# Seven-product gate and up: weight loads a tile further ahead of the hidden stores, another order of activation sums, and the second down chunk's loads amid h's

## What is computed

```python
h = h + mixed @ w_out[l]
u = rmsnorm(h, ln2_g[l])
h = h + (jax.nn.silu(u @ w_ffn_gate[l]) * (u @ w_ffn_up[l])) @ w_ffn_down[l]
```

## Time and profile before

| | us |
|---|---|
| median of 3 runs (2720.54 to 2722.23) | 2721.73 |
| the profiled execution's own time | 2721.55 |
| its span, first to last instruction | 2719.7 |
| TensorE busy | 2539.5 |
| VectorE busy | 1730.8 |
| GpSimd busy | 1062.1 |
| ScalarE busy | 944.5 |

### The profile page before, as it was taken

How to read it: one execution, slowest core, us unless ns; L and a number is a source line. 1 busy time by engine, 2 the same in 40 slices (tenths; PEclk the granted TensorE clock), 3 DMA queues, 4 the chain that set the end, 5 groups by cost and what they waited for, 6 DMA issues and landing times. The chain is left out here.

```text
span 2719.7 us, 32247 instructions
## 1 busy us (share of the span) xinstructions
PE 2539.5 (93%) x12772; PEld 1995.1 (73%) x12772; DVE 1730.8 (64%) x1757; ACT 944.5 (35%) x1380; POOL 1062.1 (39%) x555
## 2 busy tenths in 40 slices
PE   7999998998999989899999999899979999989998
PEld 5777765676777777688877777566867777777887
DVE  7777368557676666555667753965577766665554
ACT  6344156624333332100234331854243323320003
POOL 2000431156665566433520023121656655654333
PEclk9999999998999999999999999999999999999999
DMA  5010200032222322422220111002322232224221
GB/s 179 24 40 15 54 22 1 27 129 70 70 70 75 89 70 70 183 95 102 101 64 15 41 40 38 5 1 83 103 62 70 70 91 72 70 86 178 106 96 63
DMA packets 208295, 193.24 MB, mean 71 GB/s; under 512 B 31249, under 2 KB 180881, under 8 KB 208146
## 3 DMA queue, kind: packets, MB, share of 16 engines
q1 hardware_dynamic: 208146, 191.17, 22.3%
HBM read 147.11 MB, written 44.04 MB: 70 GB/s over the span
## 5 line engine op out<-in xcount | busy, mean ns | idle before, releaser
L2128 DVE TENSOR_TENSOR h<-ps,h 128x1024 f32<-128x1024 f32 x176 | 214.3, 1223 | 205.7 <-PE ps L228 191.4
L1972 POOL TENSOR_TENSOR w_a<-w_raw,w_a 128x512 fp32r<-128x512 f32 x110 | 187.7, 1731 | 371.0 <-ACT w_a L1962 371.0
L228 PE MATMUL ps<-u_hi,w_hi 128*128 128x512 f32 x896 | 295.8, 412 | 27.6 <-DVE f L872 13.3
L228 PE MATMUL ps<-u_hi,w_lo 128*128 128x512 f32 x896 | 280.0, 394 | 0.0
L228 PE MATMUL ps<-u_lo,w_hi 128*128 128x512 f32 x896 | 279.9, 394 | 0.0
L211 POOL TENSOR_TENSOR w_hi<-w_raw,ones 128x1024 fp32r<-128x1024 f32 (+1 forms) x37 | 70.2, 1898 | 482.9 <-DMA w_raw<-w_in 231.5
L2011 PE MATMUL ps<-u_b,w_a 128*128 128x512 f32 x1056 | 253.7, 389 | 0.0
L2011 PE MATMUL ps<-u_t,w_s 128*128 128x512 f32 x1056 | 246.5, 389 | 0.0
L2011 PEld LDWEIGHTS ps<-u_b,w_a 128*128 128x128 f32 x1056 | 198.2, 188 | 41.2
L2011 PEld LDWEIGHTS ps<-u_t,w_s 128*128 128x128 f32 x1056 | 198.2, 188 | 41.1
L228 PEld LDWEIGHTS ps<-u_hi,w_hi 128*128 128x128 f32 x896 | 164.0, 191 | 73.1 <-issue 24.0
(11 more groups left out here) (372 smaller groups left out, 5038.1 us busy)
## 6 DMA issues: line engine op xcount, KB each, us to landing
w_raw<-w_gate SPq DMA_DIRECT2D x44, 512.0 KB, 4.4
w_raw<-w_up SPq DMA_DIRECT2D x44, 512.0 KB, 5.5
hidden_spill<-hidden_gate SPq DMA_DIRECT2D x44, 512.0 KB, 3.3
w_raw<-w_down SPq DMA_DIRECT2D x44, 512.0 KB, 4.4
hidden_back<-hidden_spill SPq DMA_DIRECT2D x44, 512.0 KB, 4.1
w_raw<-w_in SPq DMA_DIRECT2D x42, 512.0 KB, 3.8
h_spill<-h SPq DMA_DIRECT2D x32, 512.0 KB, 4.7
h<-h_spill SPq DMA_DIRECT2D x32, 512.0 KB, 7.5
```

The lines of the kernel that those rows point to most:

```text
L228: last = nc.tensor.matmul(ps[:, bank0 + half, :], a, b[:, half * HALF:(half + 1) * HALF], start=(k == order[0] and n == 0), stop=(k == ord ...
L1972: nc.gpsimd.tensor_tensor(lo, src, hi.bitcast(F32), ALU.subtract).then_inc(w_lo, 1)
L2128: nc.vector.tensor_tensor(wide(h[:, m, :]), pair(p), wide(h[:, m, :]), ALU.add)\
```

## The change

The loads of tile i+1 move from behind the store of tile i-1 to ahead of it: the order is now load 1, load 2, store 0, load 3, store 1, and so on. A load waits for four low parts of the tile before. S3 moves to the second place of the weight order. The raws of T3 and T2 lie in the buffers of the hidden gate and up (`TRAW`), and VectorE makes T3's low parts, in another order of all activation sums. W is split from C22. At the end of the tiles, down chunk 0 is loaded ahead of the store of tile 20, the loads of chunk 1 stand after four of h's eight blocks, the last store behind all of h, and VectorE's low parts of chunk 0's hidden rows ahead of C11 of the last tile.

```diff
-        W_ORDER = ["A11", "A12", "A22", "S3", "S1", "S2", "S4"]
+        W_ORDER = ["A11", "S3", "A12", "A22", "S1", "S2", "S4"]
...
+        TRAW = [x[:, half * HALF:(half + 1) * HALF] for x in (GA, UP) for half in range(2)]
...
-                    sp.wait_ge(w_lo, 7 * i if i == 1 else 7 * (i - 1) + 3)
+                    sp.wait_ge(w_lo, 7 * i if i == 1 else 7 * (i - 1) + 4)
...
-            def dve_c22(dve, i):
+            def dve_w(dve, i):
                 dve.wait_ge(p_done, product_at(i, "P7"))
                 dve.wait_ge(v_copied, i + 1)
                 nc.vector.tensor_tensor(WT[:, :], ps[:, bank(i, "P7"), :], VC[:, :], ALU.add).then_inc(w_summed, 1)
+
+            def dve_c22(dve, i):
                 dve.wait_ge(w_summed, i + 1)
```

SyncE's program:

```diff
-                    for i in range(1, TILES):
+                    for i in range(1, 3):
                         load_weights(sp, i, 0)
                         load_weights(sp, i, 1)
-                        store_hidden(sp, i - 1)
-                    load_down(sp, 0)
+                    for i in range(3, TILES + 1):
+                        store_hidden(sp, i - 3)
+                        if i < TILES:
+                            load_weights(sp, i, 0)
+                            load_weights(sp, i, 1)
+                        else:
+                            load_down(sp, 0)
+                    store_hidden(sp, TILES - 2)
                     load_hidden(sp, 0)
-                    store_hidden(sp, TILES - 1)
                     sp.wait_ge(p_done, 7 * TILES)
                     for k in range(KT):
+                        if k == 4:
+                            load_down(sp, 1)
+                            load_hidden(sp, 1)
                         sp.dma_start(h[:, k, :], h_rows[k]).then_inc(h_back[k // 2], 16)
-                    for c in range(1, CHUNKS):
+                    store_hidden(sp, TILES - 1)
+                    for c in range(2, CHUNKS):
```

GpSimd in tile 0:

```diff
-                    pool_weight(pool, 0, W_ORDER0[5])
-                    for k in range(4):
-                        hi, lo, lo_raw = U_AT["T3"][k]
-                        pool.wait_ge(u_hi, U_HI_AT["T3", k])
-                        pool.wait_ge(u_dve, U_DVE_AT["T2 raw", k])
-                        nc.gpsimd.tensor_tensor(lo, lo_raw, hi.bitcast(F32), ALU.subtract).then_inc(u_pool, 1)
-                    pool_weight(pool, 0, W_ORDER0[6])
+                    for name in W_ORDER0[5:7]:
+                        pool_weight(pool, 0, name)
```

ScalarE in tile 0:

```diff
                     u_part("B21", 3)
+                    u_part("B22", 0)
+                    u_part("B22", 1)
                     norm_act(act, norm2, KT - 1, SQ2, None, None)
-                    act_weight(act, 0, W_ORDER0[5])
-                    for k in range(4):
-                        u_part("B22", k)
+                    for name in W_ORDER0[5:7]:
+                        act_weight(act, 0, name)
+                    u_part("B22", 2)
+                    u_part("B22", 3)
+                    act_p5(act, 0)
                     act_p1(act, 0)
-                    act_p5(act, 0)
-                    for k in range(4):
-                        u_part("T3", k)
-                    act_weight(act, 0, W_ORDER0[6])
-                    for name in ("T2", "T4"):
+                    for name in ("T3", "T2"):
                         for k in range(4):
                             u_part(name, k)
                     act.wait_ge(proj_done, J_OUT + KT + 1)
                     norm_rs(act, 0, (rs_part, 1))
+                    for k in range(4):
+                        u_part("T4", k)
+                    act_v(act, 0)
                     act.wait_ge(h_spilled, 16 * KT)
-                    for name in W_ORDER[0:3]:
-                        act_weight(act, 1, name)
-                    act_v(act, 0)
-                    for name in W_ORDER[3:7]:
+                    for name in W_ORDER:
                         act_weight(act, 1, name)
```

VectorE in tile 0 and in the turns after it (the activation parts of T3 and T2 also take their raws from `TRAW`, and `u_ready` waits on VectorE's count for all names):

```diff
-                    for k in range(4):
-                        u_part("T3 raw", k)
-                        u_part("T2 raw", k)
-                    for k in range(4):
-                        u_part("B22", k)
-                    dve_c11(dve, 0)
-                    for name in ("T4 raw", "T2", "T4"):
+                    for name in ("T3 raw", "B22", "T3", "T2 raw", "T2", "T4 raw"):
                         for k in range(4):
                             u_part(name, k)
-                    dve_sums(dve, 1, S_ORDER)
+                    u_part("T4", 0)
+                    u_part("T4", 1)
+                    dve_w(dve, 0)
+                    u_part("T4", 2)
+                    u_part("T4", 3)
+                    dve_sums(dve, 1, S_ORDER[0:1])
+                    dve_c22(dve, 0)
+                    dve_c11(dve, 0)
+                    dve_sums(dve, 1, S_ORDER[1:4])
                     dve.wait_ge(rstd_ready, 1)
-                    dve_c22(dve, 0)
                     dve_c12(dve, 0)
                     for i in range(1, TILES):
                         dve_c21(dve, i - 1)
                         if i + 1 < TILES:
                             dve_sums(dve, i + 1, S_ORDER)
+                        dve_w(dve, i)
                         dve_c22(dve, i)
+                        if i + 1 == TILES:
+                            dve_hidden(dve, 0)
                         dve_c11(dve, i)
                         dve_c12(dve, i)
-                        if i + 1 == TILES:
-                            dve_hidden(dve, 0)
```

More of the change, by code:

```diff
@@ L1804, in build @@
                  ("B11", 3), ("T1 raw", 3), ("T1", 2), ("B21", 0), ("T1", 3), ("B21", 1), ("B21", 2), ("B21", 3)] + \
-                [(b, k) for k in range(4) for b in ("T3 raw", "T2 raw")] + \
-                [(b, k) for b in ("B22", "T4 raw", "T2", "T4") for k in range(4)]
+                [(b, k) for b in ("T3 raw", "B22", "T3", "T2 raw", "T2", "T4 raw", "T4") for k in range(4)]
         U_DVE_AT = {x: n + 1 for n, x in enumerate(U_DVE)}
@@ L1974, in u_ready @@
             def u_ready(pe, name, k):
[L1975 to L1978, removed]
+                pe.wait_ge(u_dve, U_DVE_AT[name, k])
             def pe_product(pe, i, name):
@@ L2340, in u_part @@
                         scale = ln2(k) if name == "T1" else 1.0
-                        nc.scalar.activation(hi, lo_raw, ACT.Copy, scale=scale).then_inc(u_hi, 1)
+                        src = TRAW[k] if name in ("T3", "T2") else lo_raw
+                        nc.scalar.activation(hi, src, ACT.Copy, scale=scale).then_inc(u_hi, 1)
                     nc.scalar.activation(GSQ[0][:, :], YA[:, 0, :], ACT.Square).then_inc(group_sq[0], 1)
@@ L2449, in u_part @@
                             dve.wait_ge(u_hi, U_HI_AT["UG", k])
-                            nc.vector.scalar_tensor_tensor(lo_raw, h_part(k + 4, 1), ln2(k + 4),
+                            nc.vector.scalar_tensor_tensor(TRAW[k], h_part(k + 4, 1), ln2(k + 4),
                                                            h_part(k, 1), ALU.mult, ALU.subtract).then_inc(u_dve, 1)
                         elif name == "T2 raw":
-                            dve.wait_ge(u_dve, U_DVE_AT["T3 raw", k])
-                            nc.vector.scalar_tensor_tensor(lo_raw, h_part(k, 0), ln2(k),
-                                                           U_AT["T3"][k][2], ALU.mult, ALU.add)\
+                            dve.wait_ge(u_dve, U_DVE_AT["T3", k])
+                            nc.vector.scalar_tensor_tensor(TRAW[k], h_part(k, 0), ln2(k),
+                                                           TRAW[k], ALU.mult, ALU.add)\
                                 .then_inc(u_dve, 1)
@@ L2459, in u_part @@
                             nc.vector.scalar_tensor_tensor(lo_raw, h_part(k + 4, 0), ln2(k + 4),
-                                                           U_AT["T2"][k][2], ALU.mult, ALU.subtract)\
+                                                           TRAW[k], ALU.mult, ALU.subtract)\
                                 .then_inc(u_dve, 1)
@@ L2467, in u_part @@
                             dve.wait_ge(u_hi, U_HI_AT[name, k])
-                            dve.wait_ge(u_dve, U_DVE_AT["T4 raw", k])
-                            nc.vector.tensor_tensor(lo, lo_raw, hi.bitcast(F32), ALU.subtract)\
+                            if name == "T4":
+                                dve.wait_ge(u_dve, U_DVE_AT["T4 raw", k])
+                            nc.vector.tensor_tensor(lo, TRAW[k] if name in ("T3", "T2") else lo_raw, hi.bitcast(F32), ALU.subtract)\
                                 .then_inc(u_dve, 1)
```

1 line of the change is left out of this document (removed).

## The result

The changed kernel takes 2605.83 us (median of 4 runs, 2604.51 to 2606.77) against 2721.98 us for the one before on the same chip: 0.9573 of it, 95% interval 0.9556 to 0.9590, or 116.2 us less. The forecast was 2607.5. The profiled execution took 2604.51 us.

The account below looks back on a forecast made before the run. A ring through the hidden store and the next loads, not TensorE, was taken to set the steady tiles' pace. 71.8 + 14.5 + 27.7 = 114.0 us off 2721.5 gave 2607.5; range 2592 to 2638 us.

Parts of the forecast that it names:

- Part 1: Steady tiles of both layers: loads issued ahead of stores make TensorE the bound at 19.04 us a tile; 71.8 us off.
- The ring: Steady tiles: product, store, load, landing, split, P5 copy, P3, P4, product sets the pace, 20.9 and 21.0 us a tile.
- Part 2: Tile 0: operands made in a new order start P3 and P4 earlier; 6.9 and 7.6 us by layer, 14.5 together.
- The open choice: Tile 0: whether VectorE waits when it comes second to GpSimd; waits taken, gain 6.9 us, otherwise about 10.
- Part 3: Tile 21 and first down chunks: waits and slow matmuls behind them go; 27.7 us off, bounds 15 and 30.
- All three waits: TensorE's waits, layers one/two: W at P4 of tile 21 1.7/0.8, chunk 0 3.4/3.3, chunk 1 6.9/6.0 us.
- (a): Steady tiles: the stall moves to W, P4 waits 0.7 us in each of 40 tiles; about 2636 us; chance 0.12.
- (b): Tile 0 and down start find new waits of the old size, only steady tiles gain; 2650 us; chance 0.07.
- (c): Tile 0 loses nearly all its waits and no transient follows; 130 us off, 2592 us; chance 0.06.
- (d): Steady tiles: load's loop of landing, sums, splits, issue exceeds 20.9 us; about 2803 us at 24 a tile; chance 0.02.
- (e): Steady tiles: the reordering brings no earlier loads, P5's copy stays late; 2679 us; chance 0.03.
- the other doubt: Unbroken run of matmuls: the granted clock might fall there; none expected, no size or chance given.

Follow-up runs that it names:

- first run: Kernel before, with only each tile's loads moved ahead of the store of the tile before: 2642.3 us, 0.9706 of before.
- second run: Changed kernel with only the loads put back behind the store of the tile two before: 2692.4 us, 86.6 more.
- third and fourth run: Third: changed kernel with tile 0 as before, 2617.9 us. Fourth: changed kernel with the start of down as before, 2632.3 us.
- the dose after P7: Changed kernel with each load from i = 3 on also waiting for P7 of the next tile: 2641.4 us, 35.6 more.
- the wait for seven splits: Changed kernel with each load waiting for all seven low parts of the tile before instead of four: 2618.6 us, 12.8 more.
- after P1: Changed kernel with each load from i = 3 on also waiting for P1 of the next tile: 2606.7 us, 0.8 more.

## Why the prediction was right

**Part 1, loads ahead of stores: forecast 71.8, measured 72.5** from P1 of tile 1 to P1 of tile 21. The ring named in the prediction was the bound: its order alone gives the pace (first run) and takes it away (second run). The floor of 19.04 us was met to the hundredth, so the steady part is 75.8 as summed. The layout within the tile held: loads at +10.5 us (forecast +11.6), W at +11.8 (+12.4). The product ended at +3.4, not +5, because GpSimd did not hold VectorE there. The transient was charged with 2 us a layer; it is 1.6 (20.67 and 20.70 us in tile 1), P3 waiting for P5's copy as said; that is the whole 0.7.

**Part 2, tile 0: forecast 14.5, measured 14.3** (6.3 and 8.0 against 6.9 and 7.6). In the changed kernel's timeline of tile 0:

```profile
637.42 2.72 POOL L269 TENSOR_TENSOR acc<-acc,sq 128x1024 f32<-128x1024 f32 x1 [2.22 <-ACT sq L257]
...
637.80 4.59 DVE L2453 SCALAR_TENSOR_TENSOR hidden_up<-h,vectors 128x512 f32<-128x512 f32 x2
...
644.20 0.70 PE L2007 MATMUL ps<-u_b,w_hi 128*128 128x512 f32 x2 [2.90 <-DVE u_b L2446]
...
658.95 1.19 PE L2007 MATMUL ps<-u_t,w_hi 128*128 128x512 f32 x2 [2.94 <-DVE w_sum L2044]
```

P1 starts 0.72 us later in this trace than before, so 644.20 is 643.5 on the old clock (forecast 643.6), and P1 of tile 1 at 663.32 is 662.6 (662). The open choice is settled: the last two T3 raws took 4.59 us beside GpSimd's accumulation and splits where a free one takes 0.7, so the second one to come does wait. The rule of the Trainium skill ("SBUF — State Buffer", "Who interferes with whom") and this trace agree.

**Part 3, the start of down: forecast 27.7, undoing it costs 26.5.** All three waits went. The margin at chunk 1 is as worked out: its last weight part is ready at 1084.53, 2.1 us ahead of its first matmul. By the traces alone the stretch gained about 30 us (26.6 in the table and most of the 3.7 below it). The prediction put all of it down to the new start of down; the first run shows that the order of the loads gives 5.9 us of it by itself. So the total is right, and the split between parts 1 and 3 is a few us off.

**The rivals.** (a), a stall that moves to W: W is done 3.9 us ahead of P4 (810.70 against 798.23 + 16.32). (b), no gain in tile 0 and down: undoing them costs 12.1 and 26.5 us (third and fourth run). (c): tile 0's waits did not vanish, the bounds of part 2 were wide. (d), the longer ring: landings would have to be 12 us; even the dose after P7 stays below the kernel before. (e), loads no earlier: they leave 10.5 us into the tile instead of 6.4 us into the next. The clock stayed at full over the unbroken stretch, which was the other doubt; the stretch view of 340 us in the middle, busy times per engine, then the granted clock:

```profile
700.00:1040.00 340.00, 340.00 (x1502) 281.53 (x1501) 214.45 (x215) 118.97 (x198) 188.42 (x127) 1.00 0.25 82
```

The sum came out 2.2 us low (114.0 against 116.2). By the spans it is 3.1 (117.1): part 1 was 0.7 us better than its term, part 3 2.6 us, part 2 0.2 us worse.

## What to carry to other kernels

When an engine's wait repeats in every tile, follow it around until it closes; if the ring passes through an in-order queue where a transfer stands behind a later result for no need, moving that one line gives the whole gain of the steady tiles (79.8 of 116.2 us here), and nothing else in the tile has to change. Then measure how late the transfer may be: here 9.2 us into a tile was free, 11.0 was not, and the wait for seven splits cost 12.8 us through one load per layer, that of tile 2. What is freed in a ramp is partly handed back in the next tile, so the parts of such a change do not simply add: the order is worth 79.8 us alone and 86.6 when it is taken away.

## What had not been expected

VectorE's busy time per tile became shorter, though it does the same work. In the stretch of 340 us it was busy 214.5 us for 17.9 tiles, 12.0 a tile; in the kernel before, the same length holds 228.0 us for 16.3 tiles, 13.9 a tile:

```profile
720.00:1060.00 340.00, 315.77 (x1369) 256.45 (x1367) 228.01 (x195) 106.53 (x182) 202.85 (x114) 0.99 0.26 77
```

GpSimd's splits start behind P1's copy instead of with the landing, so VectorE's product and scalings (1.23 us at 800.41, 2.20 us in the earlier trace rows) run while GpSimd waits. Two engines that hold each other had been pushed into the same 14 us by the late load. The doses bear this out: with the loads later in the changed kernel, after P1 and after P7, VectorE is busy 13.2 and 14.3 us a tile (236.5 and 245.3 in the stretch 700 to 1040), and in the first run, with the early loads alone, 12.1 (215.2).

The second is the price of the transfers' neighbours: up weights landed 4.8 us after their issue (median; 5.5 before), hidden stores 2.6 us (3.3 before), now that they are not issued together. Where the store follows right behind the loads, in the doses after P1 and after P7, the loads take 4.9 and the stores 5.5 us: the one that goes second pays.
